# A two-layer decoder trunk on one core: the projection and scores of the last two retrieval heads placed behind the first round of gathered rows in phase 0

## What is computed

```
q = (xn @ w_q).reshape(T, 8, 256)                 # 8 heads, two halves of 128
s1 = einsum('thd,nd->thn', q[..., :128], sub_keys[0])
s2 = einsum('thd,nd->thn', q[..., 128:], sub_keys[1])
v1, i1 = top_k(s1, 16); v2, i2 = top_k(s2, 16)
cs, ci = top_k(v1[..., :, None] + v2[..., None, :], 16)   # of 256 pairs
experts = e1 * 128 + e2;  gates = softmax(cs)
z = einsum('td,ted->te', xn, u[experts])
out = einsum('te,ted->td', gelu(z) * gates, v[experts])
```

## Time and profile before

| | us |
|---|---|
| median of 3 runs | 1789.95 |
| lowest, highest | 1789.15, 1819.06 |
| span of the profiled execution | 1790.2 |
| PE, DVE, POOL, ACT busy in it | 1418.7, 1134.1, 1060.9, 276.2 |
| share of time the 16 DMA engines carry data, mean rate | nearly all, 361 GB/s |

### The profile page before, as it was taken

The page is one execution under the profiler, slowest core; times in us unless marked ns, Lnnn a source line. Parts: engine busy times, 40 slices in busy tenths (PEclk is TensorE's granted clock), DMA queues, the critical chain, the costliest instruction groups (busy, mean ns, idle before and its releaser), DMA issues.

```text
span 1790.2 us, 16346 instructions
## 1 busy us (share of the span) xinstructions
PE 1418.7 (79%) x5036; PEld 840.4 (47%) x5036; DVE 1134.1 (63%) x2871; ACT 276.2 (15%) x762; POOL 1060.9 (59%) x1030
## 2 busy tenths in 40 slices
PE   7987688998998678888679677888577876687766
PEld 7876444664665245544346244454336532233322
DVE  2655775765676686675558686675464858664445
ACT  1221011211111110121111111122111111111110
POOL 0005654776767655677666655577675666666664
PEclk9998898998999889998889889899798988898887
DMA  9677989999999999999999999999899899999998
GB/s 340 259 306 287 330 321 325 398 412 387 363 413 411 409 356 407 368 392 360 379 393 393 396 359 379 361 360 350 305 385 346 301 393 349 371 355 373 374 363 327
DMA packets 164241, 647.10 MB, mean 361 GB/s; under 512 B 18624, under 2 KB 18880, under 8 KB 151616
## 3 DMA queue, kind: packets, MB, share of 16 engines
q0 software_dynamic: 147456, 536.94, 78.9%
q1 hardware_dynamic: 16704, 109.17, 15.3%
HBM read 644.99 MB, written 1.05 MB: 361 GB/s over the span
## 4 chain that ended last, share of the span: by engine, by line
PE 45%; issue 15%; DVE 14%; another core or an unknown queue 12%; POOL 6%; ACT 5%; DMA 3%; ACTq 0%; POOLq 0%; DVEq 0%
PE acc L1456 23%; PE bank L1231 9%; DVE u_ring L860 6%; PE bank L1235 5%; POOL u_ring L431 3%; POOL v_ring L431 3%; ACT diag L1130 2%; PE bank L1211 2%; DMA u_ring<-in_u,idx_all 2%; PE bank L1409 1%; DMA v_ring<-in_v,idx_all 1%; ACT arena L955 1%; DVE xn L453 1%; ACT xT L940 1%
## 5 line engine op out<-in xcount | busy, mean ns | idle before, releaser
L1456 PE MATMUL acc<-v_ring,diag 128*128 128x512 f32 x1932 | 926.3, 641 | 226.2 <-ACT diag L1130 120.6
L431 POOL DMA_INDIRECT v_ring<-in_v,idx_all x512 | 533.7, 1042 | 411.8 <-PE acc L1456 198.9
L1456 PEld LDWEIGHTS acc<-v_ring,diag 128*128 128x128 f32 x1932 | 392.9, 206 | 737.5 <-issue 612.0
L431 POOL DMA_INDIRECT u_ring<-in_u,idx_all x512 | 525.2, 1026 | 306.3 <-issue 148.6
L860 DVE SCALAR_TENSOR_TENSOR u_ring<-u_ring,scp 128x1024 f32<-128x1024 f32 x272 | 319.3, 1218 | 105.3 <-DMA u_ring<-in_u,idx_all 99.2
L860 DVE SCALAR_TENSOR_TENSOR u_ring<-u_ring,xp 128x1024 f32<-128x1024 f32 x240 | 285.1, 1227 | 65.7 <-DMA u_ring<-in_u,idx_all 40.5
L874 DVE SCALAR_TENSOR_TENSOR act_w<-ez,gz 128x8 f32<-128x8 f32 x64 | 10.8, 169 | 242.9 <-ACT ez L1125 180.2
L1130 ACT ACTIVATE diag<-ident,act_w 128x128 f32<-128x128 f32 x483 | 148.4, 388 | 18.9 <-DVE act_w L874 8.3
L1235 PE MATMUL bank<-w_ring,xT 128*128 128x256 f32 x576 | 131.4, 389 | 4.9 <-ACTq L941 4.9
L1235 PEld LDWEIGHTS bank<-w_ring,xT 128*128 128x128 f32 x576 | 111.6, 195 | 23.3 <-ACTq L941 6.0
L1231 PE MATMUL bank<-xT,w_ring 128*128 128x128 f32 x896 | 112.8, 289 | 9.4 <-issue 8.0
(11 more groups left out here) (161 smaller groups left out, 973.8 us busy)
## 6 DMA issues: line engine op xcount, KB each, us to landing
w_ring<-in_wall SPq DMA_DIRECT2D x86, 1024.0 KB
u_ring<-in_u,idx_all POOLq DMA_INDIRECT x512
v_ring<-in_v,idx_all POOLq DMA_INDIRECT x512
u_ring<-in_wall SPq DMA_DIRECT2D x4, 1024.0 KB, 10.1
v_ring<-in_wall SPq DMA_DIRECT2D x3, 1024.0 KB, 8.9
arena<-in_wall SPq DMA_DIRECT2D x3, 1024.0 KB, 15.6
gains<-in_gains SPq DMA_DIRECT2D x5, 512.0 KB, 14.1
kept<-in_wall SPq DMA_DIRECT2D x2, 1024.0 KB
```

The costliest lines, as they stand in the source:

```text
L431: nc.gpsimd.indirect_dma_start(out=ring[:, r, :], out_offset=None, in_=table, in_offset=bass.IndirectOffsetOnAxis(ap=idx_all[:, slot:slot ...
L1456: ins = M(acc[:, s], diag[:, r, :], v_ring[:, r, s], start=h_last and lo + n == 0 and r == 0, stop=not h_last and hi == ROUNDS and n == hi ...
```

## The change

The projection and the scores of heads 6 and 7 in phase 0 leave their place ahead of round 0 and are worked, on PE and ACT, as the first thing of `rest`, behind round 0 and ahead of round 1. ACT counts up `projected` once behind `scores(2)` and once behind the late `scores(3)`; DVE has a fourth wait, at the key part of heads 6-7. Six chunks are lent where seven were: chunk 26 goes to the ring (as its 21st chunk, which waits for chunk 16 to be used). Every later chunk of the ring stands one place further. Since the loop of `project` no longer frees the last lent chunk, a `lent_read` of its own stands behind `queries(2)`. Other phases keep their order.

```diff
+LATE_PART = 4
-LENT, AHEAD = 7, 3
+LENT, AHEAD = 6, 3
@@ place_chunks
-            elif (layer, t) == (0, 0) and m >= LENT_FIRST:
+            elif (layer, t) == (0, 0) and LENT_FIRST <= m < LENT_FIRST + LENT:
@@ DVE, key_part
-                if p < 3:
+                if p < 3 or phase == 0 and p == LATE_PART:
                     wait_next(projected)
@@ ACT and PE, rest
-            def rest(phase):
+            def rest(phase, late):
+                if phase == 0:
+                    late()
@@ ACT, route
                 scores(2)
+                if phase == 0:
+                    act.sem_inc(projected, 1)
                 yield
                 route_part(phase, 1)
-                queries(3)
-                scores(3)
-                act.sem_inc(projected, 1)
-                yield rest(phase)
+                def late():
+                    queries(3)
+                    scores(3)
+                    act.sem_inc(projected, 1)
+                if phase:
+                    late()
+                yield rest(phase, late)
@@ PE, project
-                        if LENT_FIRST < count.chunks <= LENT_FIRST + LENT:
+                        if LENT_FIRST < count.chunks < LENT_FIRST + LENT:
                             lent_read(count.chunks - LENT_FIRST)
@@ PE, route
                 queries(2)
+                if phase == 0:
+                    lent_read(LENT)
                 scores(1)
                 scores(2)
                 yield
-                queries(3)
-                scores(3)
-                count.next(projected.name, 3)
-                yield rest(phase)
+                def late():
+                    queries(3)
+                    scores(3)
+                if phase:
+                    late()
+                    count.next(projected.name, 3)
+                else:
+                    count.next(projected.name, 4)
+                yield rest(phase, late)
```

More of the change, by code:

```diff
@@ L727, in each, with key_part @@
                         (link if op is ops[-1] and m is of[-1] else tick)(op(m))
-            def key_part(p):
+            def key_part(phase, p):
                 lo, heads = PARTS[p]
-                if p < 3:
+                if p < 3 or phase == 0 and p == LATE_PART:
                     wait_next(projected)
@@ L824, in route @@
                 count.banks += 10
-                key_part(0)
+                key_part(phase, 0)
                 pair_part(phase, 0)
@@ L828, in route @@
                 gate_part(phase, 0)
-                key_part(1)
+                key_part(phase, 1)
                 pair_part(phase, 1)
@@ L836, in rest @@
                 for p in range(2, len(PARTS)):
-                    key_part(p)
+                    key_part(phase, p)
                     yield
```

## The result

| | us |
|---|---|
| kernel before, 22 runs | median 1794.63 (1781.28 to 1819.06) |
| changed kernel, 22 runs | median 1811.53 (1786.42 to 1828.65) |
| ratio | 1.0064, interval 1.0039 to 1.0088 |
| span of the profiled execution | 1813.4 (before 1790.2) |

The change costs 0.64%: 11.5 us, 7.0 to 15.8 by the interval. The forecast was 1783.7 in a range up to 1793; within 2% of before is right, sign and range are wrong. (The ratio is that of undisturbed executions alone, while the two medians, over all 22, lie 16.9 us apart; the executions profiled here, in e10 and in e11 are disturbed ones, but the kind of stall read from them stands in undisturbed ones too, e12, e6 and e7.)

The account below looks back on a forecast made before the run. DMA stood at 8 or 9 tenths, but at 150 to 185 us a chain of waits through PE, ACT and DVE was taken to bind. Span 1790.2 - 6.3 = 1783.9, so 1783.7 us; range 1776 to 1793, its own 1777.5 to 1789.

Parts of the forecast that it names:

- Round 0 starts earlier: Round 0's tanh on ACT at 156.7, including 0.3 us of drain; PE starts round 0 at 157.7, 10.5 us earlier.
- the v rows: POOL's gathers for round 0 are issued from 153.5, the last at 159.7; PE waits for none.
- How long round 0 takes: Round 0 on PE takes 14.9 us (14.0 to 15.7, by clock level), ending at 172.6.
- The moved work: Behind round 0: 7.7 us on PE, then 4.4 us to round 1's tanh, at 184.7 instead of 191.02.
- The gain: Round 1's tanh on ACT comes 6.3 us earlier (191.02 - 184.7), and this is passed on.
- DVE's side: DVE has round 1's gelu argument zi at 180.5, 4.2 us before ACT asks for it.
- What is late next: The chain behind round 1 moves as one piece, next mixer's transposes from 212.65 to 206.3; the gain lasts.
- The loads: SP's shifted ring loads end by about 129, before the first gather; cost 0, with 2.6 us kept for the range.
- B: DMA bounds from first gather to end; earlier PE wins nothing, chunk 34's load adds 2.55 us: 1792.5; chance 0.12.
- C: Work only moved: late projection on PE at 1.2 GHz, up to 15.4 us instead of 7.7; 1788 to 1792; chance 0.1.
- D: More than forecast: a stall drops out or round 1's clock stays up, about 5 us more, 1778; chance 0.15.
- E: No effect, because the unknown stalls happen to grow by as much: 1790; chance 0.03.

Follow-up runs that it names:

- e10: e7 with POOL waiting until PE has used chunk 26 before it issues v rows 4 to 7 of round 0; starving chip; 1798.76 us, ratio 1.0051.
- e11: Changed kernel with projection and scores back ahead of round 0, still six chunks lent; starving chip; 1797.41 us, ratio 1.0015.
- e12: Changed kernel with 48 semaphore increments at the start of ACT's program; starving chip; 1814.82 us, ratio 1.0161.
- e6: Changed kernel with the projection still behind round 0 but the scores and ACT's copies behind round 1; starving chip; 1795.1 us, ratio 1.0038.
- e7: Changed kernel with the projection back at its old place on PE, only ACT's copies and eight score matmuls late; starving chip; 1802.44 us, ratio 1.0090.
- e8: e7 with seven chunks lent, as in the kernel before; starving chip; 1792.48 us, ratio 1.0014.
- e2: Changed kernel with projection and scores back ahead of round 0, still six chunks lent; fast chip; 1639.5 us, ratio 1.0007.
- e9: Changed kernel with POOL holding round 1's gathers until ACT has copied the late scores; starving chip; 1800.77 us, ratio 1.0114.
- e13: Kernel before, unchanged, on the fast chip; 1638.49 us, ratio 1.0003.
- e1: Changed kernel as it is, on the fast chip; 1642.9 us, ratio 1.0029.
- e14: e8 again, on the fast chip; 1638.54 us, ratio 1.0000.
- e4: Changed kernel with 48 semaphore increments at the start of ACT's program; fast chip; 1643.45 us, ratio 1.0032.
- e15: e7 again, on the fast chip; 1639.67 us, ratio 1.0010.

## Why the prediction was wrong, step by step

**Round 0 starts earlier, and the v rows: right.** Tanh forecast at 156.7, came at 156.56; PE at 157.7, came at 157.66; drain 0.3, was 0.30; POOL's rows at 153.5 and 159.7, were 153.29 and 159.50. Nothing waited for them.

**How long round 0 takes: 14.9, was 15.67,** the upper bound. A pause of 2.40 us ahead of it cost as much as 2.92 had; with none (e8, e10) the round takes 13.90. The Trainium skill, "TensorE: Matmul & The Clock Gate", section "What's actually happening", has recent activity release the throttled clock, from which the prediction read 14.0. This round doesn't bear that reading out (15.67 behind 2.40 us), e2's round 1 does (14.00 behind 2.39).

**The moved work: this step failed.** It was priced at 7.7 us on PE and 4.4 us for what follows, both from rows at 155 to 167 us, where DMA's share is 0.69, and set down unchanged where the share is 1.0. From 173.16 to the tanh at 200.12 it took 27.0 us, not 12.1: 14.8 on PE, 8.5 until ACT began its copy, 3.7 for the rest. Of the 14.9 us too many, 7.8 are the wait ahead of the copy, 3.8 the holes on PE, and the rest slower matmuls. e9 shows PE's price right with the gathers held (7.3 us), e12 the stall again. The rows had the warning: "unknown" stalls of 5.08 and 4.91 us, which the sum put at 5 us either way instead of asking with what they go. And before had the same projection in a full stretch, on PE's timeline:

```profile
268.62 0.61 PE L1231 MATMUL bank<-xT,w_ring 128*128 128x128 f32 x4 [0.82 <-issue]
270.04 0.60 PE L1231 MATMUL bank<-xT,w_ring 128*128 128x128 f32 x4 [0.81 <-issue]
```

Four matmuls each 1.4 us, where unhindered they take 0.5 (3.81 for 32): such rows were the bound from above, and the range left them out.

**The gain was one against stalls, too.** The forecast had round 0's tanh 10.4 us earlier and the way from there to round 1's 4.1 us longer. On the chip of the result the first came (10.55), and the second was 19.7. On the fast chip, where before has no such stall, the first is 3.35 us and the second 9.5: the change loses 6.2 us at round 1 and 1.0029 (4.8 us) at the end, though its moved work is cheaper there than priced (10.2 us from 170.09 to the tanh at 180.26, against 12.1). The rows hid this, for DVE's 23.6 us between the tanhs and PE's wait of 5.08 ahead of the projections held stalls; without them DVE's part takes 17.0 (e13).

**DVE's side: the term was right, the stalls were not.** zi forecast at 180.5; e8 has the tanh waiting for it until 181.12, but that is luck: 7.8 us of waits for u rows, which had no term, stand there in place of the two stalls of 6.9 us in the rows. In the changed kernel it came at 187.29, with 13.8 us of holes, where before had 4.91 and one of 1.95. Even without ACT's late copy that is 2.6 us behind the 184.7 of the sum.

**What is late next: not borne out.** The sum took all 6.3 us of round 1 to the end. On the fast chip e1's delay of 6.2 us at round 1 is 4.5 at the end, and on the starving chip e8 was 9.0 us ahead at round 1 and ends at 1.0014 (0.9968 to 1.0061), which leaves out even 6.3 us. So even a round 1 as early as forecast does not secure the gain at the end. In the changed kernel the transposes stand at 217.29, not 206.3. Against before, its 9.1 us at round 1 are 5.6 at round 2 and 11.3 at round 5; the stalls are dealt anew each time, and one profile can't say more.

**The loads: right on one chip** (e2: 1.0007, at most 1.0016). On the other the six lent chunks let four gathers go 3 us sooner, and these starve the kept chunk's matmuls where they stand at their old place (e7 against e8 and e10, e11).

**The rivals.** B (DMA sets the end) is wrong in that PE's order counts (e1 against e2, in the medians); its 2.55 us for the added load lie within e2's interval, and its claim that an earlier PE wins nothing came true in e14, by way of u rows that DVE waited for, and in e8, where a stall took part of it. C put the price at 1.2 GHz. The granted clock is 1.00 from 173 to 177 and 0.67 from 177 to 182, behind the first holes, and it costs at least 2.9 us of the 14.8 on PE (the kept chunk's 5.42 against 3.81, ten matmuls' 2.50 against 1.2). C had the right place and the smaller part of the mechanism, and its matmuls slowed down behind holes, where it had none. D (more than forecast) did not come. E's words, that the unknown stalls grow, come nearest, and had 0.03. The range was also added up too narrow: its own terms (0.8, 0.3, 2.6 and 5 us) reach 1792.4, not 1789.

**What stays open:** what the engines wait for. The Trainium skill, "Runtime: NRT & Kernel Launch", section "Instruction fetch mechanics", says that each engine's sequencer fetches its instructions in blocks by a DMA queue of its own while it works the last ones, and that this is mostly hidden. It fits that one matmul at a time gets through and that gathers decide; the traces of the fast chip, without a hole in this stretch, agree with it, and on the other chip it would not be hidden. But it is argued: of the 81 packets of the two "instruction" queues on the page of the changed kernel only three fall between 150 and 202 us (at 160, 176 and 188), where PE and DVE alone have seven holes, and no run changed them. Why one chip starves and another doesn't is open too.

## What to carry to other kernels

Before work is moved out of the way of something, look whether the engine that does it would have been idle there: without stalls only 3.65 us could be won in front of round 0, and behind it all of the work is in the open. A gain at one round is not yet a gain at the end (e8, e14). A duration belongs to its surroundings; work that goes from a stretch with free DMA into one with saturated gathers is priced by rows of a stretch like that one (the two rows of L1231 above). And stalls that the profile can't name are a resource to be understood first: ask beside what they stand, and whether another chip has them.

## What the runs showed of the hardware

- The same kernel takes 1638 us on two chips (e1 to e4, e13 to e15) and 1787 to 1795 us in the three other sets of runs. From 140 us on, DMA carries 404 GB/s at a share of 1.01 on the first (e13) and 368 GB/s at 0.96 on the other; there 109 us of ACT's idle time ahead of its copies of L955 are put down to "remote" (the profile of before), on the first none. Idle time is not all stall: ACT's 36.93 us ahead of 196.38 hold 8.5 us of it.
- Starved work has a pattern of its own: on PE one matmul (0.27 or 0.37 us) every 0.7, 1.4 or 2.1 us with "issue" between (e7, e6), on DVE single waits of 1.3 to 6.6 us (the changed kernel), on ACT a copy that comes 5.5 to 12.1 us after what it needs is complete (e11, e12, e8, the changed kernel, e10). It is gone where the gathers are held (e9), and holding four gathers until chunk 26 was used kept PE's kept chunk free of it once (e10).
- A round of 32 matmuls takes 13.90 to 13.97 us straight behind PE's unbroken work (e8, e10, e14), 15.81 straight behind starved work (e7; granted clock 0.61 from 162 to 175) and 15.48 behind a pause of 7.59 (e1). Behind a pause of 2.0 to 2.4 us both come: 14.00 (e2's round 1, 2.39) and 15.36 or 15.67 (e2's round 0, 2.02; the changed kernel, 2.40). The granted clock is 0.50 in parts of such stretches (158 to 162 of e9: 0.57 on the mean), the lower of the two levels; what decides at 2 us these runs don't show.
